# First attention of a three-layer block on one Trainium2 core: output products on two column halves, softmax weights normed by GpSimd before they are turned

## The chip, the cores and the metric

One core of one Trainium2 chip runs the whole program. The metric is the device time of one execution in microseconds (us), as the median of the runs. Engines are TensorE (PE in the profile, its weight loads PEld), VectorE (DVE), ScalarE (ACT), GpSimd (POOL) and SyncE (SP, which issues most transfers).

## The reference

256 tokens of width 1024, all in float32, pass through three layers. The change lies in the first one, an attention with 16 heads of 64 features and one shared key and value head (k and v of 64 features each, 256 keys):

```
q = rms_norm(proj_q per head);  k = rms_norm(proj_k);  v = proj_v
allowed = the 64 best keys by an indexer's score, in chunks not later than the query's
logits = (q . k) / 8 + rel_bias[t5_bucket(key - query)];  -1e30 where not allowed
p = softmax(logits);  out = p @ v;  h = h + out(256 x 1024) @ w_o
h = h + (relu(norm(h) @ w_up) ** 2) @ w_down
```

## The kernel before

**Blocks.** Tokens lie in two blocks of 128 rows. Queries of block 0 see only keys 0 to 127, those of block 1 all 256. So the softmax weights of one head are 128 x 384 numbers: 128 x 128 of block 0 and 128 x 256 of block 1, side by side in a buffer `P` (four heads deep), queries on the partitions.

**Per head.** TensorE makes the logits of two heads at a time (`logits_a`, L1079: row halves of 64 features, then a bf16 product that adds the mask). DVE adds the bias from `A["toep"]`, writes minus the logits to `P` and takes the row minimum in the same instruction (`min_a`, L2764). ACT takes the exponential in place, and its sum per row into `den` (L2037). TensorE turns three 128 x 128 blocks (L716, called from `turned`, L891) into a PSUM bank, 6 or 7 by turns. DVE copies them to `PT` (`turned`, L2720); ACT does so for heads 7, 10 and 13 (`act_turns`, L330). Then three products with the turned weights stationary and 64 value columns moving (L904 to L906) give the output with tokens on the partitions:

```
o0, o1 = psum[:, g % 2, at:at + 64], psum[:, g % 2, 256 + at:256 + at + 64]
nc.tensor.matmul(o0, pt[:, 0:128], vcol(0, h), start=True, stop=True)
nc.tensor.matmul(o1, pt[:, 128:256], vcol(0, h), start=True, stop=False)
ins = nc.tensor.matmul(o1, pt[:, 256:384], vcol(1, h), start=False, stop=True)
```

**Per group of four heads.** DVE takes the reciprocals of `den` and scales the group's output (`normed_out`, L2725). TensorE turns it (`out_turned`, L910), ACT makes the high half (`out_high`, L2017) and DVE the low half (`out_low`, L2734) of a two-part representation: each large product is made as three (high x high, high x low, low x high; L628 to L630). The product with w_o goes in four weight chunks wo0 to wo3; chunk j takes group j's output (`product`, L915).

**Order.** Every engine's program is written out by hand. TensorE's (`attention`, L888) takes logits two pairs ahead of the transposes, and spreads the first quarters of chunk wo0's product into the last heads. Engines meet by semaphores only; each engine runs its instructions in order.

**Weight chunks.** SP loads a chunk of 1 MB; its high half is made by ACT (L1769), or by GpSimd for the names in `pool_high` (wo1 and wo2 here), its low half by DVE (L2417) or GpSimd (L1726). GpSimd's program also scales the queries (`scale_queries`, L1690): the second half of them at the start of the attention. A chunk's buffer is loaded again once its low half is made.

**Other work around it.** TensorE makes a table `tab_c` (24 x 512) for a later layer at the start of the attention; ACT copies it out (L2060) and stores it, and issues, behind its last head (L2050, L1925), a 3 MB transfer that writes it shifted row by row to `skew_c` in HBM. The first MLP follows: its second kind of weights (`mlp0.d0`) is loaded once the low half of `mlp0.u0` is made.

**The dilated attention.** In the third layer's attention (L1419) the values are stationary, 64 columns to a head, two heads on the two column halves of the array, and the output has features on the partitions.

Of the kernel before, what the change touches and what calls it, by code (L numbers as in the profile page):

```python
# [23 lines left out]
P = 128  # L24
# [84 lines left out]
def program(nc, t):  # L109
# [8 lines left out]
    with ctx:  # L118
# [89 lines left out]
        for j in range(4):  # L208
            rows(f"wo{j}", kview(t["a_w_o"][0]), 2 * j, 2, D, lo="dve" if j == 3 else "pool")
# [120 lines left out]
        act_turns = {"A": (7, 10, 13), "B": (1, 7, 10, 13)}  # L330
# [76 lines left out]
        plan("a_exp_ready", [f"A.h{h}.exp" for h in range(16)])  # L407
        plan("b_row_max", [f"B.h{h}.max" for h in range(16)])
# [73 lines left out]
        def hidden_count(s, p, k):  # L482
# [9 lines left out]
             "score": area(8592, NB, SEQ), "P": area(9104, 4, 384), "PT": area(10640, 2, 384),  # L492
             "o": area(12304, 4, 512), "toep": area(14352, 16, SEQ)}
# [47 lines left out]
        hs, hd, hr = st[:, 8:40], st[:, 40:72], st[:, 72:104]  # L541
        mx, nmx, den, rden = st[:, 104:112], st[:, 112:120], st[:, 120:152], st[:, 152:184]
# [64 lines left out]
        def _(pe):  # L607
# [343 lines left out]

            logit_bank = (4, 5, 2, 3)
# [150 lines left out]
            def between_a(i, part):  # L1103
                if (i, part) == (1, 0):
                    query_transposes(1, (6, 7))
                if (i, part) == (2, 0):
                    wait_read("A.qT2")
                    wait_read("A.qT3")

            attention("A", logits_a, lambda s, h: A["kvw"][:, s, 64:128], "wo", between_a)  # L1110
# [522 lines left out]
        def _(pool):  # L1633
# [63 lines left out]

            for c in range(NC):
                if chunks[c]["name"] in ("wo0", "wo1"):
                    scale_queries(int(chunks[c]["name"][2]))  # L1700
                if chunks[c]["name"] == "dqb":
# [48 lines left out]
        def _(act):  # L1750
# [271 lines left out]
            def turned(L, h):  # L2022
                S = A if L == "A" else B
                act.wait_ge(*full[f"{L}.h{h}.T"])
                run(S["PT"][:, h % 2, :], psum[:, bank[f"{L}.h{h}.T"], 0:384], ACT.Copy, read[f"{L}.h{h}.T"])

            def heads(L, tag, between, behind=0):
                split_at = {"A": {6: 1, 10: 2}, "B": {5: 0, 8: 1, 11: 2}}[L]
                for h in range(16):
# [4 lines left out]
                    for blk, c0, w in ((0, 0, 128), (1, 128, 256)):  # L2034
                        at, c = (h // 4) * 8 + blk * 4 + h % 4, (h % 4) * 2 + blk
                        if L == "A":
                            run(A["P"][:, h % 4, c0:c0 + w], A["P"][:, h % 4, c0:c0 + w], ACT.Exp,  # L2037
                                done[f"A.h{h}.exp"] if blk else None, bias=mx[:, c:c + 1], scale=-1.0,
# [1198 lines left out]
```

## Time and profile before

| what | value |
|---|---|
| median of 3 runs | 1105.88 us (1105.83 to 1105.90) |
| the profiled execution's own time | 1105.73 us |
| its span | 1103.6 us |
| TensorE busy | 1090.9 us, 99% of the span |
| DVE, ACT, GpSimd busy | 757.8, 600.3, 149.6 us |
| granted TensorE clock over the span | 0.999 |
| first attention, from the first exponential to the third chunk of w_o | about 60 to 99 us |

The share of busy time is an average over the whole program. Matmuls are pipelined and their ends are modelled, so the way from one TensorE line to the next is read from starts; a product on f32 operands is recorded as two instructions.

### The profile page before, as it was taken

Reading aid. Unit: us, or ns where it says so; the run is one execution under the profiler, and the core shown is the slowest. Engines: PE = TensorE matmul, PEld = TensorE weight load, DVE = VectorE, ACT = ScalarE, POOL = GpSimd, SP = SyncE. Lnnn points to the kernel's source line nnn. Section 1 sums busy time; section 2 is a strip of 40 time slices with the busy share of each in tenths; the row PEclk is TensorE's granted clock in tenths of the full one; section 3 lists DMA queues with packets and bytes.
Section 4 is the critical chain, followed back from the end, with each engine's and each line's share of the span. In section 5 each row is a group of like instructions: output and inputs, shape, how many; then the busy total and the mean of one; then the engine's idle time right before and its main releaser. Section 6 shows DMA issues by size and latency. Waiting matters only on the chain.

```text
span 1103.6 us, 17798 instructions
## 1 busy us (share of the span) xinstructions
PE 1090.9 (99%) x6977; PEld 973.0 (88%) x6977; DVE 757.8 (69%) x1054; ACT 600.3 (54%) x788; POOL 149.6 (14%) x113
## 2 busy tenths in 40 slices
PE   8999999999999999999999999999999999999997
PEld 7868888888998888888889999898899989999997
DVE  6774665656668466656557878576587577988884
ACT  6574644444698464444455546555555357546454
POOL 4652000000377220000030000000000002000003
PEclk9999999999999999999999999999999999999999
DMA  9836565556433156565645654446653556545631
GB/s 303 289 117 123 188 223 191 191 190 233 138 106 129 33 161 217 187 195 189 200 154 191 191 158 144 131 153 231 201 166 121 168 214 229 200 176 196 226 136 39
DMA packets 138929, 194.00 MB, mean 176 GB/s; under 512 B 7163, under 2 KB 113112, under 8 KB 138860
## 3 DMA queue, kind: packets, MB, share of 16 engines
q1 hardware_dynamic: 129004, 184.02, 50.7%
q10 hardware_dynamic: 9248, 8.95, 3.2%
q8 instruction: 47, 0.77, 0.3%
q0 software_dynamic: 608, 0.08, 0.1%
q14 instruction: 22, 0.18, 0.0%
HBM read 191.90 MB, written 6.37 MB: 180 GB/s over the span
## 4 chain that ended last, share of the span: by engine, by line
PE 91%; ACT 4%; DVE 4%; issue 1%; DVEq 0%; ACTq 0%
PE psum L628 22%; PE psum L629 22%; PE psum L630 22%; PE psum L842 11%; PE psum L846 6%; ACT arena L1755 3%; PE psum L716 2%; PE psum L746 1%; PE psum L1392 1%; PE psum L1419 1%; DVE arena L2711 1%; DVE st L2710 1%; PE psum L1353 0%; PE psum L904 0%; PE psum L906 0%
## 5 line engine op out<-in xcount | busy, mean ns | idle before, releaser
L2417 DVE TENSOR_TENSOR wlo<-raw,whi 128x2048 fp32r<-128x2048 f32 (+1 forms) x134 | 302.4, 2264 | 134.8 <-ACT whi L1769 133.7
L1769 ACT ACTIVATE whi<-raw 128x2048 fp32r<-128x2048 f32 (+1 forms) x149 | 277.4, 1871 | 174.0 <-PE psum L630 126.3
L628 PE MATMUL psum<-xA,whi 128*128 128x256 f32 x840 | 239.2, 285 | 0.0
L630 PE MATMUL psum<-xA,wlo 128*128 128x256 f32 x840 | 237.6, 283 | 0.0
L629 PE MATMUL psum<-xA,whi 128*128 128x256 f32 x840 | 237.6, 283 | 0.0
L1726 POOL TENSOR_TENSOR wlo<-raw,whi 128x288 fp32r<-128x288 f32 (+3 forms) x43 | 81.8, 1930 | 746.5 <-ACT whi L1769 746.2
L628 PEld LDWEIGHTS psum<-xA,whi 128*128 128x128 f32 x840 | 160.3, 191 | 2.9 <-DVE wlo L2648 0.9
L629 PEld LDWEIGHTS psum<-xA,whi 128*128 128x128 f32 x840 | 160.4, 191 | 1.1
L630 PEld LDWEIGHTS psum<-xA,wlo 128*128 128x128 f32 x840 | 160.3, 191 | 0.1
L842 PE MATMUL psum<-xA,whi 128*128 128x512 f32 x512 | 122.5, 390 | 0.0
L628 PE MATMUL psum<-whi,xC 128*128 128x512 f32 (+1 forms) x296 | 114.5, 387 | 0.0
L629 PE MATMUL psum<-wlo,xC 128*128 128x512 f32 (+1 forms) x296 | 114.2, 386 | 0.0
L630 PE MATMUL psum<-whi,xC 128*128 128x512 f32 (+1 forms) x296 | 113.9, 385 | 0.0
L842 PEld LDWEIGHTS psum<-xA,whi 128*128 128x128 f32 x512 | 95.5, 188 | 20.7 <-DVE xA L2525 1.3
L628 PE MATMUL psum<-whi,xA 128*128 128x512 f32 (+1 forms) x256 | 99.9, 390 | 0.0
L630 PE MATMUL psum<-whi,xA 128*128 128x512 f32 (+1 forms) x256 | 98.3, 384 | 0.0
L629 PE MATMUL psum<-wlo,xA 128*128 128x512 f32 (+1 forms) x256 | 98.2, 384 | 0.0
L1890 ACT ACTIVATE arena<-psum 128x512 f32<-128x512 f32 x32 | 19.1, 597 | 96.1 <-PE psum L846 96.0
L846 PEld LDWEIGHTS psum<-xA,wlo 128*128 128x128 f32 x512 | 65.6, 191 | 2.5
L846 PE MATMUL psum<-xA,wlo 128*128 128x256 f32 x512 | 66.4, 283 | 0.0
L630 PEld LDWEIGHTS psum<-whi,xC 128*128 128x128 f32 x296 | 55.6, 188 | 10.8
L628 PEld LDWEIGHTS psum<-whi,xC 128*128 128x128 f32 x296 | 55.7, 188 | 9.8
(311 smaller groups left out, 1685.7 us busy)
## 6 DMA issues: line engine op xcount, KB each, us to landing
raw<-in_w_in SPq DMA_DIRECT2D x42, 1024.0 KB, 5.0
raw<-in_mlp_w_up SPq DMA_DIRECT2D x32, 1024.0 KB, 5.3
raw<-in_mlp_w_down SPq DMA_DIRECT2D x32, 1024.0 KB, 4.8
raw<-in_w_gate SPq DMA_DIRECT2D x11, 1024.0 KB, 5.2
raw<-in_w_up SPq DMA_DIRECT2D x11, 1024.0 KB, 6.4
down_raw<-in_w_down SPq DMA_DIRECT2D x6, 1024.0 KB, 8.1
arena<-in_w_down SPq DMA_DIRECT2D x5, 1024.0 KB, 8.3
raw<-in_b_w_o SPq DMA_DIRECT2D x4, 1024.0 KB, 5.0
```

The costliest lines, as they stand in the source:

```text
L628: nc.tensor.matmul(out, lh, rh, start=start, stop=False, skip_group_check=skip)
L629: nc.tensor.matmul(out, lh, rl, start=False, stop=False, skip_group_check=skip)
L630: return nc.tensor.matmul(out, ll, rh, start=False, stop=stop, skip_group_check=skip)
L716: ins = nc.tensor.transpose(out[0:m, n * P:n * P + P], src, ident[:, :])
L746: ins = nc.tensor.transpose(out[:, (2 * i + blk) * P:(2 * i + blk) * P + P], hres[:, blk, k * P:k * P + P], ident[:, :])
L842: nc.tensor.matmul(psum[:, 4 + 2 * j2 + nt, :], hi[:, k, nt * P:nt * P + P], xA[:, :, k, :], start=k == 0, stop=False)
L846: ins = nc.tensor.matmul(psum[:, 4 + 2 * j2 + nt, 0:SEQ], lo[:, k, nt * P:nt * P + P], xA[:, 0, k, :], start=False, stop=k == KT - 1)
L1726: ins = T(wlo[split_of[c]][:, at:at + step], raw_bufs[raw_of[c]][:, at:at + step], f(whi[split_of[c]][:, at:at + step]), ALU.subtract)
L1755: ins = nc.scalar.activation(out, in_, func, **kw)
L1769: nc.scalar.activation(whi[split_of[c]][:, 0:n], raw_bufs[raw_of[c]][:, 0:n], ACT.Copy).then_inc(hi_sem, 1)
L1890: nc.scalar.activation(half_buf[:, j2, :].rearrange("p (a b) -> p a b", b=SEQ), psum[:, 4 + 2 * j2:6 + 2 * j2, SEQ:512], ACT.Copy).then_in ...
L2417: V.tensor_tensor(wlo[split_of[c]][:, 0:n], raw_bufs[raw_of[c]][:, 0:n], f(whi[split_of[c]][:, 0:n]), ALU.subtract).then_inc(lo_sem["dve"], 1)
```

## The change

- The output products of the first attention keep the values stationary (128 x 64) and move the turned weights (256 columns of the first key block, 128 of the second). Even heads write partitions 0 to 63, odd heads 64 to 127. The output is feature-major at once, so its transposes and the scaled copy on DVE are gone.
- As tokens now lie along the columns, the weights are normed before they are turned: DVE takes the reciprocals of a pair (`weight_factor`), GpSimd scales `P` in place (`norm_weights`), two instructions a head. DVE does it all for heads 0 and 1.
- The turned weights of a pair are copied in one instruction of 128 x 768 from banks 6 and 7, by DVE, or by ACT for pairs 3, 5 and 7. `P` is six heads deep, `PT` four, the row minima eight.
- GpSimd splits wo1 in pieces between the pairs. It makes wo2's high half behind them; wo2's low half is DVE's.
- `tab_c` is copied by DVE instead of ACT. The transposes of the second half of the queries come ahead of head 0's. ACT's shifted store to `skew_c` stands behind its copy of pair 7.

The diff, cut to its core. First the chunk list, TensorE's program and GpSimd's:

```diff
-            rows(f"wo{j}", kview(t["a_w_o"][0]), 2 * j, 2, D, lo="dve" if j == 3 else "pool")
+            rows(f"wo{j}", kview(t["a_w_o"][0]), 2 * j, 2, D, lo="dve" if j >= 2 else "pool")
...
+        act_pairs = (3, 5, 7)
...
+            def attention_pairs(logits, value, tag, between):
+                def turned(h):
+                    if h % 2 == 0:
+                        open_bank(f"A.t{h // 2}", 7)
+                        pe.wait_ge(read_sem[6], uses[6])
+                    pe.wait_ge(*done[f"A.h{h}.nrm" if h > 1 else f"A.h{h}.first"])
+                    for n in range(3):
+                        ins = nc.tensor.transpose(psum[:, 6 + h % 2, n * P:n * P + P],
+                                                  A["P"][:, h % 6, n * P:n * P + P], ident[:, :])
+                    if h % 2:
+                        close_bank(ins, f"A.t{h // 2}")
...
+                def outputs(i):
+                    g, at, pair = i // 2, (i % 2) * 256, (2 * i, 2 * i + 1)
+                    if i % 2 == 0:
+                        open_bank(f"A.oT{g}", g % 2)
+                    wait_read(f"A.t{i}")
+                    for k, c0, w, p0 in ((0, 0, 256, 0), (1, 128, 128, 256)):
+                        for h in pair:
+                            r0 = (h % 2) * 64
+                            ins = nc.tensor.matmul(psum[r0:r0 + 64, g % 2, at + c0:at + c0 + w], value(k),
+                                                   A["PT"][:, h % 4, p0:p0 + w], start=k == 0, stop=k == 1,
+                                                   skip_group_check=True)
+                    if i % 2:
+                        close_bank(ins, f"A.oT{g}")
...
+                for i in range(7):
+                    between(i, 0)
+                    if i < 6:
+                        logits(i + 2)
+                    if i == 0:
+                        query_transposes(1, (0, 1))
+                    if i == 1:
+                        outputs(0)
+                    turned(2 * i)
+                    if i > 1:
+                        outputs(i - 1)
+                    turned(2 * i + 1)
+                    if i == 6:
+                        open_residual(tag, (0, 2))
+                        product(0, (0, 2))
+                turned(14)
+                outputs(6)
+                turned(15)
+                open_residual(tag, (1, 3))
+                product(0, (1, 3))
+                outputs(7)
+                product(1, (0, 1, 2, 3))
+                product(2, (0, 1, 2, 3))
+                last_residual_step(tag, "M0", xA, lambda j: read[f"A.oT{j}"])
...
+            def norm_weights(i):
+                pool.wait_ge(*done[f"A.rden{i}"])
+                for h in (2 * i, 2 * i + 1):
+                    for blk, c0, w in ((0, 0, 128), (1, 128, 256)):
+                        at = (h // 4) * 8 + blk * 4 + h % 4
+                        p = A["P"][:, h % 6, c0:c0 + w]
+                        ins = nc.gpsimd.tensor_scalar(p, p, rden[:, at:at + 1], None, ALU.mult)
+                        if blk:
+                            ins.then_inc(done[f"A.h{h}.nrm"][0], 1)
...
+            def weighted_heads():
+                c = split_started("wo1")
+                for i in range(1, 3):
+                    run(high_piece(c, 1024 * (i - 1), 1024))
+                    norm_weights(i)
+                for i in range(3, 7):
+                    ins = low_piece(c, 512 * (i - 3), 512)
+                    if i == 6:
+                        ins.then_inc(lo_sem["pool"], 1)
+                    norm_weights(i)
+                norm_weights(7)
+                c = split_started("wo2")
+                run(high_piece(c, 0, 1024))
+                run(high_piece(c, 1024, 1024), done["wo2.hi"])
...
```

ScalarE's program:

```diff
+            def turned_pair(i):
+                act.wait_ge(*full[f"A.t{i}"])
+                run(A["PT"][:, (2 * i) % 4:(2 * i) % 4 + 2, :], psum[:, 6:8, 0:384], ACT.Copy, read[f"A.t{i}"])
...
-                    if L == "A" and h - 2 in act_turns["A"]:
-                        turned("A", h - 2)
-                    if h - behind in (8, 12):
+                    if L == "A" and h % 2 and (h - 3) // 2 in act_pairs:
+                        turned_pair((h - 3) // 2)
+                    if L == "A" and h in (7, 11):
+                        out_high(L, (h - 7) // 4)
...
                 if L == "A":
+                    turned_pair(7)
                     act.wait_ge(s_tab, 32)
                     shift_rows(tab_c, skew_c, 24)
...
```

VectorE's program:

```diff
+            def turned_pair(i):
+                dve.wait_ge(*full[f"A.t{i}"])
+                if i not in act_pairs:
+                    run(V.tensor_copy(A["PT"][:, (2 * i) % 4:(2 * i) % 4 + 2, :], psum[:, 6:8, 0:384]), read[f"A.t{i}"])
...
+            def first_weights_normed(h):
+                dve.wait_ge(*done[f"A.h{h}.exp"])
+                run(V.reciprocal(rden[:, h:h + 5:4], den[:, h:h + 5:4]))
+                for blk, c0, w in ((0, 0, 128), (1, 128, 256)):
+                    p = A["P"][:, h, c0:c0 + w]
+                    run(V.tensor_scalar(p, p, rden[:, h + 4 * blk:h + 4 * blk + 1], None, ALU.mult),
+                        done[f"A.h{h}.first"] if blk else None)
+
+            def head_pairs(row_min, between):
+                for i in range(8):
+                    if i == 0:
+                        row_min(4)
+                        turned_pair(0)
+                        row_min(5)
+                    else:
+                        for h in (2 * i + 4, 2 * i + 5):
+                            if h < 16:
+                                row_min(h)
+                        turned_pair(i)
+                    if i < 7:
+                        weight_factor(i + 1)
+                    between(i)
+                    if i in (4, 6):
+                        out_low("A", (i - 4) // 2)
+                low_of("wo2")
+                out_low("A", 2)
+                low_of("wo3")
+                out_low("A", 3)
...
             min_a(2)
-            heads("A", min_a, between_a)
+            dve.wait_ge(*full["tab_c"])
+            run(V.tensor_copy(lrow_c, psum[0:24, bank["tab_c"], :]), read["tab_c"])
+            min_a(3)
+            first_weights_normed(0)
+            first_weights_normed(1)
+            head_pairs(min_a, between_a)
```

`weight_factor(i)` waits for the exponential of head 2i + 1 and takes the four reciprocals of pair i; `between` holds DVE's scaled copy of the fourth query tile at i = 0.

## Rows read from the trace of the kernel before

**Rows 1.** The page, chain that ended last: share of the span by engine.

```profile
PE 91%; ACT 4%; DVE 4%; issue 1%; DVEq 0%; ACTq 0%
```

**Rows 2.** Windows: us; busy us (instructions) of PE, PEld, DVE, ACT, POOL; clock, DMA, GB/s.

```profile
60.00:70.00 10.00, 8.76 (x71) 6.15 (x67) 6.98 (x27) 7.45 (x26) 9.65 (x7) 1.00 0.63 217
...
80.00:90.00 10.00, 10.00 (x78) 9.35 (x79) 6.50 (x20) 5.19 (x18) 0.00 (x0) 1.00 0.14 28
```

**Rows 3.** Timeline, transposes of heads 0 and 3: start us, us, engine, line, what.

```profile
61.35 0.55 PE L716 MATMUL psum<-ident,arena 128*128 128x128 f32 x3 [0.46 <-ACT arena L1755]
...
67.28 0.55 PE L716 MATMUL psum<-ident,arena 128*128 128x128 f32 x3
```

**Rows 4.** Timeline of one pair: logits, mask, transposes, DVE's copy, next transposes.

```profile
68.06 0.39 PE L906 MATMUL psum<-arena 128*128 128x64 f32 x2
...
68.37 0.93 PE L1087 MATMUL psum<-arena 64*128 64x128 f32 x8
...
69.23 0.50 PE L1091 MATMUL psum<-pick_mask,ident_bf 128*128 128x384 bf16 x2
...
69.57 0.49 PE L716 MATMUL psum<-ident,arena 128*128 128x128 f32 x3
...
70.16 0.56 DVE L2723 COPY arena<-psum 128x384 f32<-128x384 f32 x1 [0.64 <-PE psum L716]
...
70.61 0.55 PE L716 MATMUL psum<-ident,arena 128*128 128x128 f32 x3
```

**Rows 5.** Chain in order of time, the same transposes: end of chain step, us, line.

```profile
69.73 0.34 PE psum L716 x3
```

**Rows 6.** Timeline: transposes of heads 13 and 15, first wo2 product.

```profile
83.54 0.50 PE L716 MATMUL psum<-ident,arena 128*128 128x128 f32 x3
...
88.19 0.50 PE L716 MATMUL psum<-ident,arena 128*128 128x128 f32 x3
...
99.03 0.39 PE L628 MATMUL psum<-whi,xA 128*128 128x512 f32 x1
```

**Rows 7.** Timeline of the dilated attention: its output products on column halves.

```profile
802.70 2.17 PE L1419 MATMUL psum<-arena 128*64 128x256 f32 x24
804.71 0.61 PE L1425 MATMUL psum<-ident,st 128*64 128x128 f32 x8
```

**Rows 8.** Groups by form, whole program: count, busy us, mean ns, idle before.

```profile
L1721 POOL CAST whi<-landing 128x1024 fp32r<-128x1024 f32 x2 | 2.1, 1038 | 0.1
L1726 POOL TENSOR_TENSOR wlo<-raw,whi 128x512 fp32r<-128x512 f32 x16 | 19.9, 1276 | 24.1 <-ACT whi L1769 23.8
L2723 DVE COPY arena<-psum 128x384 f32<-128x384 f32 x25 | 13.9, 558 | 7.3 <-PE psum L716 6.7
L1755 ACT ACTIVATE arena<-psum 128x384 f32<-128x384 f32 x27 | 13.3, 491 | 16.2 <-PE psum L716 15.2 <-ACT arena L1755 0.5
L3027 DVE TENSOR_SCALAR arena<-arena,st 128x256 f32<-128x256 f32 x8 | 3.3, 413 | 0.3
L2769 DVE CUSTOM_DVE_ANT_0 arena<-psum,arena 128x256 f32<-128x256 f32 x16 | 6.8, 424 | 0.6
```

**Rows 9.** Timeline: skew_c transfer, load of mlp0.d0, its high half, its first product.

```profile
86.34 0.85 ACTq L1925 DMA_DIRECT2D skew_c<-tab_c  x1
...
105.94 0.37 SPq L1531 DMA_DIRECT2D raw<-in_mlp_w_down  x1
...
116.12 1.92 ACT L1769 ACTIVATE whi<-raw 128x2048 fp32r<-128x2048 f32 x1 [1.72 <-DMA raw<-in_mlp_w_down]
...
123.25 0.45 PE L628 MATMUL psum<-whi,xC 128*128 128x512 f32 x1
```

**Rows 10.** DMA queues (packets, MB, share) in 86.0:101.1, then 105.9:113.4; q10 is skew_c.

```profile
q10 hardware_dynamic: 1896, 1.94, 66.2%
...
q10 hardware_dynamic: 485, 0.49, 41.9%
q1 hardware_dynamic: 240, 0.81, 41.3%
```

More of the change, by code:

```diff
@@ L407, in program @@
         plan("a_exp_ready", [f"A.h{h}.exp" for h in range(16)])
+        plan("a_factor_ready", [f"A.rden{i}" for i in range(1, 8)])
+        plan("a_first_weights_normed", [f"A.h{h}.first" for h in range(2)])
+        plan("a_weights_normed", [f"A.h{h}.nrm" for h in range(2, 16)])
+        pool_high_ready = plan("pool_high_ready", ["wo2.hi"])
         plan("b_row_max", [f"B.h{h}.max" for h in range(16)])
@@ L1700, in _ @@
                     scale_queries(int(chunks[c]["name"][2]))
+                if chunks[c]["name"] == "wo1":
+                    weighted_heads()
+                    continue
                 if chunks[c]["name"] == "dqb":
@@ L2022, in turned @@
             def turned(L, h):
[L2023 removed]
                 act.wait_ge(*full[f"{L}.h{h}.T"])
[L2025 removed]
+                run(B["PT"][:, h % 2, :], psum[:, bank[f"{L}.h{h}.T"], 0:384], ACT.Copy, read[f"{L}.h{h}.T"])
+            def turned_pair(i):
+                act.wait_ge(*full[f"A.t{i}"])
+                run(A["PT"][:, (2 * i) % 4:(2 * i) % 4 + 2, :], psum[:, 6:8, 0:384], ACT.Copy, read[f"A.t{i}"])
             def heads(L, tag, between, behind=0):
[L2028 removed]
+                split_at = {"A": {}, "B": {5: 0, 8: 1, 11: 2}}[L]
                 for h in range(16):
@@ L2036, in heads @@
                         if L == "A":
-                            run(A["P"][:, h % 4, c0:c0 + w], A["P"][:, h % 4, c0:c0 + w], ACT.Exp,
-                                done[f"A.h{h}.exp"] if blk else None, bias=mx[:, c:c + 1], scale=-1.0,
+                            c = (h % 8) * 2 + blk
+                            run(A["P"][:, h % 6, c0:c0 + w], A["P"][:, h % 6, c0:c0 + w], ACT.Exp,
+                                done[f"A.h{h}.exp"] if blk else None, bias=row_mins[:, c:c + 1], scale=-1.0,
                                 accum_out=den[:, at:at + 1])
@@ L2055, in between_a @@
             def between_a(h):
-                if h == 2:
+                if h == 3:
                     query_turned(2)
                 if h == 4:
-                    act.wait_ge(*full["tab_c"])
-                    run(lrow_c, psum[0:24, bank["tab_c"], :], ACT.Copy, read["tab_c"])
+                    act.wait_ge(*read["tab_c"])
                     act.dma_start(tab_c.ap(), lrow_c).then_inc(s_tab, 16)
@@ L2414, in low_part @@
             def low_part(c, hi_value=None):
-                dve.wait_ge(hi_sem, high[c] if hi_value is None else hi_value)
+                if c == index["wo2"]:
+                    dve.wait_ge(*done["wo2.hi"])
+                else:
+                    dve.wait_ge(hi_sem, high[c] if hi_value is None else hi_value)
                 n = chunks[c]["n"]
```

57 lines of the change are left out of this document (34 added, 23 removed).

## The prediction

> **What bounds the kernel now.** I read the page first: TensorE carries 91% of the chain that ended last, and the profiled execution spans 1103.6 us [rows 1]. It took 1105.73 us by its own time, so 2.1 us lie around the span, and it stands 0.15 us under the median of the runs shown. The sum below is made against 1105.73. A measurement of this kernel can tell about 0.2% (2.2 us) from no change.
>
> Then the windows of the first attention, which runs from about 60 to 99 us. The reader is to see two things [rows 2]: TensorE has gaps in the first ten microseconds (8.76 busy of 10) and none between 80 and 90, and its granted clock is 1.00 (2.4 GHz) in both. So in its steady part the attention is bound by TensorE's own instruction stream, and what is taken from that stream is worth its time, as long as nothing else comes to stand in front of it.
>
> Then the timeline of one pair of heads [rows 4]. Logits and mask take from 68.37 to 69.57 (1.20 us; 1.29 with the 0.09 that lie before them, the last of two output records having started at about 68.17 and each taking 0.11). From 69.57 to 70.61 come three transposes, 0.34 on the chain [rows 5], and a head's three output products: 0.70. Products of 64 columns at 0.23 us each pay for loading 128x128 transposed weights, not for columns. A pair costs 1.29 + 0.67 + 1.37 (six products) = 3.3 us, and the stream from the transposes of head 3 (67.28, [rows 3]) to those of head 13 (83.54, [rows 6]) takes 16.26 us for five pairs.
>
> **The change, part by part.**
>
> Outputs on column halves. The products at 802.70 in the dilated attention have the new form: 12 of them, two heads on two column halves, 6 of 256 and 6 of 128 columns, in 2.01 us to the next line at 804.71 [rows 7]. That is 2304 columns at 0.87 ns. A pair of the first attention has 2 x 256 + 2 x 128 = 768 columns: 0.67 us. I add 0.09 on either side for the change of tile form, since the logits, which also change it, start 0.09 us after the last output product: 0.86 us for a pair against 1.37. Eight pairs give 8 x 0.51 = 4.1 us less on TensorE. The Trainium skill (TensorEngine Tiling (Array Packing), Key Properties) says that a change of the tiling mode drains the engine. The logits' own exit costs 0.22 us (0.64 by 768 columns, against 0.86 until the mask at 69.23); at 0.22 on either side the term would be 2.1 us less. I keep 0.09, the one gap that stands between two tile forms without a mask behind it, and leave the 2.1 to the range.
>
> The outputs come out feature-major, so the four blocks of output transposes go, 0.45 us each (four transposes at 0.11 [rows 5]), 1.8 us. The output norm on DVE (four reciprocals and four 128x512 products) goes too; it was never on TensorE's path, so nothing.
>
> In all TensorE would issue 5.9 us less. This is what would come if nothing were late.
>
> The start. DVE now copies the table rows (about 0.7), takes the row minimum of head 3 (0.8; the 256-column part is 0.42, [rows 8]), and norms heads 0 and 1 itself: a reciprocal (some 0.2) and two scalings, 0.41 and about 0.29 [rows 8], 1.0 us a head with gaps. Queued from 60.4, that puts the first transposes at 62.9 instead of 61.35 and head 1's at 63.9. Behind them stand a pair copy, a row minimum, the factor and the GpSimd norm of heads 2 and 3: head 3's transposes come to 68.2, against 67.28 [rows 3]. Loss 0.9 us.
>
> The new wait. In DVE's program the factor of pair i+1 stands behind the copy of pair i, and the copy behind the last transposes of pair i. GpSimd norms only after the factor, and the transposes of pair i+1 wait for GpSimd. So a loop goes round once a pair. From the start of a pair's last transposes: 0.59 us until the copy starts (69.57 to 70.16, [rows 4]); the copy of 768 columns 0.96 (0.56 for 384, at 1.04 ns a column more, [rows 8]); factor 0.25 (an estimate: a few columns, and the way between two engines); 0.08 to GpSimd; GpSimd's first head G; 0.05; then transposes 0.34 and outputs 0.86 on TensorE before the next last transposes. TensorE can put only the logits (1.29) under the middle of it. G has no row. Bounds: a cast has 1.04 us for 1024 columns, a two-input operation 1.28 for 512 [rows 8]. By the cast (one input, as here) with 0.18 fixed, 128 and 256 columns are 0.29 + 0.40 = 0.7; by the two-input line 0.45 + 0.72 = 1.2; 0.5 if two instructions overlap. I take 0.7, since the new operation reads one tensor. The loop is then 0.59 + 1.0 + 0.25 + 0.08 + 0.7 + 0.05 + 0.34 + 0.86 = 3.87 us where DVE copies (pairs 0, 1, 2, 4, 6). Where ACT copies (3, 5, 7) DVE only waits for the transposes, the 1.0 falls out and the ACT copy (about 0.85, from 0.49 for 384 columns, [rows 8]) lies beside the norm: TensorE's own stream binds, 2.87 us. From head 3 to head 13: 4.1 + 3.87 + 2.87 + 3.87 + 2.87 = 17.6 us (the first has 0.25 more, DVE being behind with the fourth query tile). Before: 16.3. So head 13's transposes start at 85.8 instead of 83.54: 2.2 us late, where TensorE's stream alone would have been early.
>
> The end of the attention. From head 13's transposes to the third weight product (wo2) the stream before took 99.03 - 83.54 = 15.5 us [rows 6]. In the new one there is no wait left, since the first half product (2.7 us) lies over the last norm: 0.34 + 2.73 + 0.34 + 0.86 + 0.34 + 2.73 + 0.86 + 5.46 = 13.7. Gain 1.8 us.
>
> GpSimd's and DVE's other work. The split of wo1 is spread between the norms: 1.1 to 1.3 us a piece, against 1.5 to 2.5 us in which GpSimd waits each turn; nothing. It is whole before the second product. The low part of wo2 moves to DVE, 2.3 us behind GpSimd's 2.1 us of high part: ready about 5 us after head 15's transposes, needed 9.4 after; nothing. ACT's split of wo3 keeps its place.
>
> So wo2's product starts 0.4 us later than before (2.2 - 1.8).
>
> The skewed bias rows. ACT issues the 3 MB transfer of skew_c at 86.34, 12.7 us ahead of wo2's product [rows 6, 9]. In the new program it stands behind the copy of pair 7, 1.5 us after head 15's transposes instead of 1.85 before them (88.19), and the stream from there is shorter: 8 us ahead. It moves 4.7 us closer to the first down weights of the MLP, whose load is issued at 105.94 behind a release that keeps its distance to wo's products. That load takes 10.2 us now because the tail of skew_c is still moving: 0.49 MB of it beside 0.81 MB of weights from 105.9 on [rows 10]. With 4.7 us less of a start, 1.2 MB are left instead. And there is no slack: the weights land at 116.12, and ACT's half, DVE's half, the square and its low part follow on, and TensorE takes them up at 123.25 without a gap [rows 9]. In the shared stretch the weights move at about 0.16 MB/us, which brings the megabyte through in 8 to 11 us. I take 1.0 us of delay; the bounds are nothing, and 4.7 if the load had to wait out the whole shift.
>
> Sum: 0.9 + 1.3 - 1.8 + 1.0 = 1.4 us; 1105.73 + 1.4 = 1107.1, beside the median about 1107.2. I give **1107.1**, 0.1% more: no change that can be told.
>
> **Rivals.**
>
> B, TensorE's saving comes whole. If the loop were shorter than I read it (the copy starting earlier, G at 0.5), TensorE's 5.9 us less would stand against 0.9 at the start and 1.0 of the transfer: 1101.7. For it: the last windows show TensorE bound [rows 2]. Against it: 0.59 and the copy's slope are read directly, and G at 0.5 alone gives 1.0 of the loop back (1106.1). Chance 0.15.
>
> C, GpSimd becomes the bound, on the other side. The place is the norm of the first head of a pair; it decides from G = 0.9 on. At the two-input price of 1.2 each loop, ACT's too, grows by 0.5, and so does the start: 6 x 0.5 = 3.0 us, 1110.1. For it: all GpSimd arithmetic in this trace but the casts goes at that price. Against it: the casts, with one input, take half. The Trainium skill (GPSIMD Engine Reference, When to use GPSIMD) calls GpSimd the wrong place for elementwise work, about twice VectorE's time for two inputs and near line rate for one; DVE's 0.41 for 256 columns beside the cast's slope agrees with the second half, and the first half is this rival. Chance 0.22.
>
> D, the bias rows collide with the down weights for most of the shift: 3 to 4.7 us of delay instead of 1.0, 1109 to 1110.8. For it: 10.2 us now against no slack at 123.25. Against: in the shared stretch the weights moved faster than the bias rows. Chance 0.12.
>
> E, the column halves don't run beside each other after transposes of the whole array: 1.4 us a pair, 1110.5. The rows at 802.70 speak against it. Chance 0.03. A fall of the granted clock in the new gaps is in none of them: at 8.76 of 10 it stayed at 1.00 [rows 2].
>
> **How the numbers follow.** Forecast 0.48, B 0.15, C 0.22, D 0.12, E 0.03. Its own range is 1105.2 to 1108.2. B gives most of faster (0.17 with a little of the forecast's edge), C, D and E nearly all of slower (0.35), the rest is the same, 0.48. The range leaves out B's end and the worst of C with D together: 1103.4 to 1110.5.
>
> **What would show it.** Outputs: a pair of heads near 0.86 us between transposes; more than 1.2 is E. The loop: TensorE idle about 1.0 us ahead of the first transposes of pairs 2, 3 and 5 (behind a GpSimd instruction), and none to speak of ahead of 4 and 6; if none anywhere, it is B. G: GpSimd's 256-column norm near 0.4; near 0.7 is C. Head 13's transposes near 85.8, wo2's product near 99.4. The transfer: the down weights land 11 us after issue and TensorE waits about 1 us before the first down product. The prediction is wrong if head 13's transposes start before 84.

## The result, and the profile after

The changed kernel takes 1118.39 us (median of 4 runs, 1117.59 to 1118.63) against 1105.89 us: ratio 1.0109, 95% interval 1.0096 to 1.0122. It is slower by 12.5 us, outside the range. The profiled execution took 1118.37 us and spans 1116.6 us.

The page, chain by engine, answers to [rows 1]. GpSimd and the DMA are new on it:

```profile
PE 87%; DVE 4%; ACT 4%; POOL 2%; issue 1%; DMA 1%; DVEq 0%; ACTq 0%; POOLq 0%
```

The timeline of TensorE, transposes of heads 0, 1, 3, 13 and 15, the wo2 product and the first down product, answers to [rows 3, 6, 9]. The first number is the start in us:

```profile
63.99 0.52 PE L966 MATMUL psum<-ident,arena 128*128 128x128 f32 x3 [0.57 <-DVE arena L2852]
...
64.81 0.55 PE L966 MATMUL psum<-ident,arena 128*128 128x128 f32 x3 [0.30 <-DVE arena L2852]
...
70.80 0.44 PE L966 MATMUL psum<-ident,arena 128*128 128x128 f32 x2 [0.87 <-POOL arena L1765]
...
95.40 0.90 PE L966 MATMUL psum<-ident,arena 128*128 128x128 f32 x3
...
101.24 0.55 PE L966 MATMUL psum<-ident,arena 128*128 128x128 f32 x3
...
110.88 0.39 PE L634 MATMUL psum<-whi,xA 128*128 128x512 f32 x1
...
136.57 0.47 PE L634 MATMUL psum<-whi,xC 128*128 128x512 f32 x1 [1.31 <-DVE xC L2721]
```

That splits the loss (starts after minus starts before, each stretch less the one ahead of it):

| stretch | before | after | change | forecast |
|---|---|---|---|---|
| to head 3's transposes | 67.28 | 70.80 | +3.5 | +0.9 |
| head 3 to head 13 | 16.26 | 24.60 | +8.3 | +1.3 |
| head 13 to the wo2 product | 15.49 | 15.48 | 0.0 | -1.8 |
| wo2 to the first down product | 24.22 | 25.69 | +1.5 | +1.0 |

The sum is 13.3; the spans differ by 13.0. Half a microsecond of the first row is there before the changed part begins (the logits of head 1 start at 56.92 instead of 56.42). Behind the first down product nothing is lost.

One turn of the loop where DVE copies, pairs 4 and 5 (heads 8 to 11), in the timeline of the four engines (to be held beside [rows 4]):

```profile
86.24 0.55 PE L966 MATMUL psum<-ident,arena 128*128 128x128 f32 x3
...
89.81 0.52 PE L966 MATMUL psum<-ident,arena 128*128 128x128 f32 x3 [1.74 <-POOL arena L1765]
90.26 0.87 PE L980 MATMUL psum<-arena 128*64 128x256 f32 x8
91.20 0.55 PE L966 MATMUL psum<-ident,arena 128*128 128x128 f32 x3
...
94.01 0.52 PE L966 MATMUL psum<-ident,arena 128*128 128x128 f32 x3 [2.25 <-POOL arena L1765]
...
86.90 0.96 DVE L2839 COPY arena<-psum 128x768 f32<-128x768 f32 x1 [1.47 <-PE psum L966]
87.89 0.18 DVE L2845 RECIPROCAL st<-st 128x4 f32<-128x4 f32 x1
...
91.84 0.18 DVE L2845 RECIPROCAL st<-st 128x4 f32<-128x4 f32 x1 [1.45 <-issue]
...
88.17 2.98 POOL L1765 TENSOR_SCALAR arena<-arena,st 128x128 f32<-128x128 f32 x4 [0.74 <-DVE st L2845]
91.11 1.27 POOL L1773 TENSOR_TENSOR wlo<-landing,whi 128x512 fp32r<-128x512 f32 x1
92.36 2.99 POOL L1765 TENSOR_SCALAR arena<-arena,st 128x128 f32<-128x128 f32 x4
```

From 86.24 to 91.20 the reader can add: 0.66 to the copy, 0.99 for it, 0.28 for the factor and the way to GpSimd, 1.49 for head 10's scaling (half of 2.98), 0.15 to the transposes, 0.45 for them, 0.94 for the outputs: 4.96 us where 3.87 stood. The odd head's scaling ends almost on the same path: GpSimd is done with head 11 at 88.17 + 2.98 = 91.15, 0.05 ahead of its transposes. From 91.20 to 95.40, where ACT copies, it is 4.20 where 2.87 stood: there the copy falls out (4.96 - 0.99 = 3.97), and GpSimd's piece of wo1, running until 92.38, holds the scaling up by another 0.2. The outputs are busy for 0.87, about the 0.86 forecast; they are not at fault.

The windows of after show a second loss, which [rows 2] don't have (columns as there; the last three are granted clock, DMA share and GB/s):

```profile
68.00:70.00 2.00, 0.52 (x3) 0.31 (x3) 1.81 (x9) 1.38 (x6) 2.00 (x4) 1.00 0.00 0
70.00:72.00 2.00, 1.20 (x9) 1.03 (x11) 0.54 (x1) 1.47 (x6) 1.73 (x2) 0.82 0.00 0
72.00:74.00 2.00, 1.69 (x8) 0.35 (x4) 1.03 (x5) 0.00 (x0) 1.20 (x2) 0.50 0.02 4
...
76.00:78.00 2.00, 2.00 (x13) 1.18 (x11) 0.26 (x1) 1.06 (x3) 1.01 (x1) 0.50 0.00 0
...
88.00:90.00 2.00, 0.26 (x3) 0.22 (x3) 1.83 (x9) 1.13 (x5) 1.83 (x3) 1.00 0.00 0
...
92.00:94.00 2.00, 0.00 (x0) 0.02 (x1) 0.02 (x1) 1.90 (x6) 2.00 (x4) 1.00 0.00 0
94.00:96.00 2.00, 1.96 (x15) 1.38 (x15) 0.00 (x0) 0.94 (x4) 1.34 (x2) 0.79 0.00 0
96.00:98.00 2.00, 2.00 (x7) 1.61 (x6) 1.53 (x3) 0.00 (x0) 0.33 (x1) 0.50 0.00 0
```

Twice, behind a gap (0.52 busy of 2 us, then 0.00 of 2), the granted clock falls to 0.50, the lower of its two levels (1.2 GHz). The Trainium skill (TensorE: Matmul & The Clock Gate, Part 1) says that an engine left idle is taken down to that level; these rows agree on the level. They don't show that every such gap is followed by a fall: from 88 to 90 us the engine was busy for 0.26 us, and the clock stayed at 1.00 up to 94.

### The profile page after: what moved, and what is told of

Read it like the earlier page. It is cut to its first block, busy times and chain, and to the rows that moved or that the text cites. A ratio compares the mean times of both kernels' runs of the same rounds, so it can differ in the third digit from the quotient of the medians.

```text
span 1116.6 us, 17718 instructions
## 1 busy us (share of the span) xinstructions
PE 1092.1 (98%) x6929; PEld 967.1 (87%) x6929; DVE 757.7 (68%) x1053; ACT 600.5 (54%) x787; POOL 166.4 (15%) x143
## 4 chain that ended last, share of the span: by engine, by line
PE 87%; DVE 4%; ACT 4%; POOL 2%; issue 1%; DMA 1%; DVEq 0%; ACTq 0%; POOLq 0%
PE psum L634 21%; PE psum L635 21%; PE psum L636 21%; PE psum L848 10%; PE psum L852 5%; ACT arena L1858 3%; PE psum L722 1%; POOL arena L1765 1%; DMA raw<-in_mlp_w_down 1%; PE psum L1452 1%; PE psum L1479 1%; ACT whi L1872 1%; PE psum L752 1%; DVE arena L2823 1%; DVE st L2822 1%
## 5 line engine op out<-in xcount | busy, mean ns | idle before, releaser
L634 PEld LDWEIGHTS psum<-whi,xC 128*128 128x128 f32 x296 | 55.7, 188 | 11.3 <-issue 1.5
```

The lines of the kernel that those rows point to most:

```text
L634: nc.tensor.matmul(out, lh, rh, start=start, stop=False, skip_group_check=skip)
```

## The experiments

Theory 1 was that GpSimd's scaling stands in a ring through each pair at twice the price taken. The rivals were a late factor, the copy, the clock and the bias rows. The runs are called m1 and e1 to e12, the changed kernel's profile is called after. A ring is a chain of waits that comes back to its start once a pair.

**GpSimd's price by itself (m1)**, in the kernel before, at 77 to 90 us, where GpSimd is idle.

```diff
+for n in (128, 256, 384, 512, 1024): tensor_scalar(to[:, 0:n], from[:, 0:n], column, mult)
+for n in (128, 256): tensor_scalar(... 0.5 ...), tensor_tensor of 2 x n with a repeated factor, tensor_copy, tensor_tensor
```

> The kernel before, with single GpSimd instructions on scratch columns added in GpSimd's idle time behind the splits of wo2 (75 to 100 us): a scaling by a column of scalars at 128, 256, 384, 512 and 1024 columns, by a constant at 128 and 256, a product of two tensors with one broadcast along the columns at 2x128 and 2x256, a copy at 128 and 256, a product of two whole tensors at 128 and 256. It measures the disputed price by itself. Theory 1 (the scaling by a column is dear in itself): 0.60 and 0.92 us at 128 and 256 columns here too, with nothing else going on, and the slope of a two-input operation or worse. Rival (it is dear in the changed kernel only because VectorE and GpSimd share a way into SBUF): 0.3 and 0.4 us here, near the copy. The broadcast product should take about 0.6 and 1.04 us. The time of the kernel stays at 1105.9.

Measured, groups by form (mean ns of one is the number behind the bar's second comma):

```profile
L1705 POOL TENSOR_SCALAR arena<-arena,st 128x256 f32<-128x256 f32 x1 | 0.9, 930 | 0.1
...
L1705 POOL TENSOR_SCALAR arena<-arena,st 128x128 f32<-128x128 f32 x1 | 0.6, 606 | 0.0
L1707 POOL TENSOR_SCALAR arena<-arena 128x128 f32<-128x128 f32 x1 | 0.5, 530 | 0.1
...
L1712 POOL COPY arena<-arena 128x256 f32<-128x256 f32 x1 | 0.4, 402 | 0.1
L1712 POOL COPY arena<-arena 128x128 f32<-128x128 f32 x1 | 0.3, 292 | 0.1
```

A copy costs 0.29 + 0.40 = 0.7 us, the figure taken from the cast. Scaling by a column costs 0.61 + 0.93 = 1.54 us, more than a product of two tensors (0.45 + 0.73); with a constant for the column 0.53 + 0.86. So reading one tensor is not what makes the cast cheap. The Trainium skill (GPSIMD Engine Reference, When to use GPSIMD) calls work with one input on GpSimd roughly line-rate. Here that holds for the copy alone: 256 columns in 0.40 us, where DVE's scaling took 0.41 [rows 8] and GpSimd's takes 0.93.

**The scaling left out (e1), and cut to one column (e2).** The first leaves out the scaling of heads 2 to 15, the second all but the first column of each block.

```diff
-pe.wait_ge(*done[f"A.h{h}.nrm" if h > 1 else f"A.h{h}.first"])
+pe.wait_ge(*done[f"A.h{h}.exp" if h > 1 else f"A.h{h}.first"])
...
 def norm_weights(i):
+    return
```

```diff
-p = A["P"][:, h % 6, c0:c0 + w]
+p = A["P"][:, h % 6, c0:c0 + 1]
```

> The changed kernel without GpSimd's norm of heads 2 to 15: the softmax weights of these heads stay unnormed, and TensorE's transposes wait for the exponential instead. Theory 1 (the norm is what was lost): TensorE's stream binds, about 2.9 us a pair; head 13's transposes start near 80 us of the span instead of 95.4, and the time is about 1102 to 1103 us, with the load of the first down weights still 1 to 2 us late. Rival (the clock, or the pair copies and the order of VectorE's queue, hold TensorE back without any norm): 1108 us or more.

> The changed kernel with every wait and every GpSimd instruction of the norm, but each scales one column instead of 128 or 256; the other weights stay unnormed. Theory 1 (the loop is as predicted and only GpSimd's duration was mis-sized): with about 0.3 us an instruction a head costs 0.6, the loop is near the predicted 3.9 and 2.9 us, and the time is the predicted one, 1106 to 1108 us. Rival (the order of the queues is what costs, whatever the norm takes): above 1112 us. Second rival (gaps of 1 us a pair already halve the clock): above 1110 us, with the granted clock under 1.0 in the stretch from 70 to 100 us.

Measured 1108.77 us (ratio 1.0024, 1.0015 to 1.0034) and 1109.23 us (1.0028, 1.0018 to 1.0038). Between 9 and 10 us go, so the scaling is the main cause. In the second a head's scaling takes 0.52 us (1.04 for four instructions), and TensorE still waits 4.8 us in all for GpSimd ahead of its transposes. From head 3 (about 68.7) to head 13 (86.46) it is 17.8 us. The forecast's 17.6, worked out again with 0.52 for 0.7 in its three turns with a copy by DVE, would be 17.1: at such a price the ring is within 0.7 us of the one foretold. The clock stays at 1.00 from 60 to 112 us, so gaps of 0.8 to 1.3 us did not lower it. Its time still lies 1.2 us above the 1106 to 1108 expected, and the first missed its 1102 to 1103 us by 6. The timeline of DVE and GpSimd in the first says why:

```profile
64.15 2.05 DVE L2845 TENSOR_SCALAR arena<-arena,st 128x128 f32<-128x128 f32 x2
66.23 0.17 DVE L2842 RECIPROCAL st<-st 128x2 f32<-128x2 f32 x1
66.44 2.34 DVE L2845 TENSOR_SCALAR arena<-arena,st 128x128 f32<-128x128 f32 x2
...
63.91 2.14 POOL L1763 CAST whi<-landing 128x1024 fp32r<-128x1024 f32 x2
66.14 4.99 POOL L1766 TENSOR_TENSOR wlo<-landing,whi 128x512 fp32r<-128x512 f32 x4
```

DVE's scaling of heads 0 and 1 takes 2.05 and 2.34 us while GpSimd runs (the first ends at 66.20, the casts at 66.05); alone it took 0.68. GpSimd, freed of the weights, had moved its splits beside DVE. Head 3's transposes then start near 73.4. From there to head 13's it is 15.0 us.

**No scaling at all (e5)**: also DVE's of heads 0 and 1 left out.

```diff
 def first_weights_normed(h):
     run(V.reciprocal(...))
+    return
     for blk, c0, w in ((0, 0, 128), (1, 128, 256)):
```

> The changed kernel with no scaling of the weights at all, neither GpSimd's nor DVE's of the first two heads (the outputs are left unnormed); the factors of pairs 1 to 7 are still formed. In the run with only GpSimd's scaling left out, DVE's two scalings of the first heads took 2.05 and 2.34 us instead of 0.68 us beside GpSimd's splits of the next weights, TensorE waited 1.35 and 1.97 us for them and its clock was 0.50 of full in 70 to 72 us. Theory (that stretch is why the run missed its 1102 to 1103 us): without them the third head's transposes start before 69 us, no clock below 1.00 from 60 to 100 us, and 1102 to 1104.5 us. Rival (the pair loop is no shorter than the loop before even without a scaling, because of DVE's copies or the bank pair): 1106 us or more, with waits for DVE copies ahead of outputs in each pair.

Measured 1104.39 us, ratio 0.9982 (0.9972 to 0.9991), at the edge of the 1102 to 1104.5 expected. This bounds the idea: with a scaling that costs nothing the new shape gives 1.7 us, and 1.28 us of wait for the down weights stand against it. In steady pairs TensorE takes 2.9 us (odd heads' transposes at 72.19, 75.13 and 78.02), as forecast (2.87), but the stretch from head 3 (67.8) to head 13 (84.22) still takes 16.4 us: TensorE has new waits for the pair copies. In the program one pair of PSUM banks carries all transposes, and one copy frees both, which is likely why; no run changed that. The timeline of TensorE:

```profile
70.91 0.55 PE L966 MATMUL psum<-ident,arena 128*128 128x128 f32 x3 [1.19 <-DVE arena L2832]
...
82.94 0.55 PE L966 MATMUL psum<-ident,arena 128*128 128x128 f32 x3 [0.96 <-ACT arena L1851]
```

**The factors first (e3).** DVE forms the factors of pair i+1 ahead of the copy of pair i.

```diff
-                        turned_pair(i)
-                    if i < 7:
-                        weight_factor(i + 1)
+                        if i < 7:
+                            weight_factor(i + 1)
+                        turned_pair(i)
```

> The changed kernel with VectorE's reciprocals of pair i+1 ahead of its copy of pair i, so that GpSimd's norm of the next pair runs under the transposes and the copy of this one. Nothing is left out. Theory 1: GpSimd itself binds now, 2.98 us of norm and 1.27 of split a pair, 4.3 us against 4.9 on average before; the time falls by about 3 us, to 1115. Rival (the order of VectorE's queue was the cause): the loop opens and the time falls below 1109.

Measured 1113.26 us, ratio 1.0061 (1.0044 to 1.0078). The copy leaves the ring and 5 us go, 2 more than expected. What is left is GpSimd itself, busy without a pause, in these windows of it (GpSimd is the fifth busy time):

```profile
80.00:82.00 2.00, 1.16 (x10) 0.44 (x8) 0.75 (x5) 1.90 (x6) 2.00 (x4) 1.00 0.00 0
82.00:84.00 2.00, 1.79 (x14) 1.10 (x14) 0.89 (x5) 1.50 (x5) 2.00 (x3) 1.00 0.00 0
```

2.98 us of scaling and a 1.27 us piece of wo1 make a turn of 4.2 us (transposes of heads 6, 8 and 10 at 77.94, 82.14 and 86.34). Now GpSimd is the bound, without any ring.

**A cheaper scaling (e4).** A pair in two products of two tensors, the factors repeated.

```diff
-for h in (2 * i, 2 * i + 1): for blk ...: tensor_scalar(P[:, h % 6, c0:c0 + w], rden[:, at:at + 1])
+for blk ...: tensor_tensor(P[:, h % 6:h % 6 + 2, c0:c0 + w], up2(rden[:, at:at + 2], w))
```

> The changed kernel with the GpSimd scaling of a pair written as two multiplies of two tensors, one for each query block of both heads, the factors repeated along the columns, instead of four multiplies by a column. The same is computed. In the run of the kernel before with added GpSimd instructions these forms took 0.62 and 1.04 us against 0.61 and 0.93 us twice each, so 1.7 instead of 3.0 us a pair. Theory 1 (the scaling's own duration stands on the path of each pair): 7 x 1.3 us go, and the two stretches at half clock (4 to 5 us) shrink or go with the gaps: 1106 to 1110 us, transposes of head 15 at 91 to 94 us instead of 101.2. Rival (the wait is for the factor, which DVE gives late behind a pair copy, and the duration only fills a part of it): the gaps stay, above 1114 us.

Measured 1116.69 us, ratio 1.0093 (1.0069 to 1.0117). A pair costs 1.61 us instead of 2.98, and next to nothing comes of it: 1106 to 1110 was wrong. The turns at full clock, from even head to even head, say why:

```profile
80.88 0.52 PE L966 MATMUL psum<-ident,arena 128*128 128x128 f32 x3 [1.55 <-POOL arena L1765]
...
84.79 0.52 PE L966 MATMUL psum<-ident,arena 128*128 128x128 f32 x3 [0.82 <-POOL arena L1765]
...
89.70 0.52 PE L966 MATMUL psum<-ident,arena 128*128 128x128 f32 x3 [1.82 <-POOL arena L1765]
```

They take 3.91 and 4.91 us, where 4.20 and 4.96 stood. Only the first head's 1.49 us were in the ring; the second head's lay beside transposes and outputs (1.39 us), and now both must end before the first transposes, 1.61. The 7 x 1.3 us expected had counted hidden time. Since both heads are ready at once, the next transposes come 1.25 us later (82.13, forecast 0.34 + 0.86 = 1.20) and not 1.39, which gives back the 0.12 that 1.61 costs over 1.49.

**The bias rows earlier (e6).** ScalarE issues skew_c ahead of head 12's exponential.

```diff
+                if h == 12:
+                    act.wait_ge(s_tab, 32); shift_rows(tab_c, skew_c, 24)
...
                     turned_pair(7)
-                    act.wait_ge(s_tab, 32)
-                    shift_rows(tab_c, skew_c, 24)
```

> The changed kernel with ScalarE issuing the second table's shifted transfer ahead of the exponentials of head 12 instead of behind the last pair copy (some 10 us earlier, to an idle time of the DMA engines). Theory (the transfer runs beside the load of the first down weights, which then comes 1 to 1.5 us late and leaves a wait of 1.3 us ahead of the first down product): the wait goes, -1.0 to -1.5 us. Rival (the load is late from its own start and the product's wait comes from DVE's low part): the wait stays, within 0.4 us of the changed kernel.

Measured 1117.28 us, ratio 1.0091 (1.0075 to 1.0108) against 1.0109. In after, the timeline shows the transfer's issue, the load's, and its landing, where ACT waits for it:

```profile
102.72 0.85 ACTq L2028 DMA_DIRECT2D skew_c<-tab_c  x1
...
117.86 0.37 SPq L1591 DMA_DIRECT2D raw<-in_mlp_w_down  x1
...
129.47 1.92 ACT L1872 ACTIVATE whi<-raw 128x2048 fp32r<-128x2048 f32 x1 [3.21 <-DMA raw<-in_mlp_w_down]
```

and with the transfer issued earlier:

```profile
87.46 0.85 ACTq L2028 DMA_DIRECT2D skew_c<-tab_c  x1
...
118.34 0.37 SPq L1591 DMA_DIRECT2D raw<-in_mlp_w_down  x1
...
126.63 1.90 ACT L1872 ACTIVATE whi<-raw 128x2048 fp32r<-128x2048 f32 x1
```

The weights are split 8.3 us after issue instead of 11.6, and the wait of 1.31 us is gone. The trace shows that; the two times alone don't, as their intervals overlap.

**The gaps filled (e7).** Eight transposes of the identity into unused columns ahead of each even head's wait.

```diff
+if h > 1 and h % 2 == 0:
+    for _ in range(8): nc.tensor.transpose(psum[:, 6, 384:512], ident[:, :], ident[:, :])
 pe.wait_ge(*done[f"A.h{h}.nrm" ...])
```

> The changed kernel with eight transposes of the identity into unused columns of the pair's first bank, ahead of the wait for each even head's scaled weights (heads 2 to 14). They take about 0.8 us of TensorE's time in gaps of 1 to 2 us. Theory (the clock fell to half after the gaps at 68 to 70 and 92 to 94 us, in stretches of 3 to 6 us): the granted clock stays 1.00 from 60 to 105 us, and the time falls by 2 to 4.5 us to 1114 to 1116.5 us. Rival (the clock falls for another reason, or such transposes don't count): the clock's rows stay as they are, and the time is the same or up to 5 us more where the transposes don't fit in the gaps.

Measured 1115.95 us, ratio 1.0086 (1.0069 to 1.0103). Its windows:

```profile
72.00:78.00 6.00, 5.07 (x41) 3.38 (x40) 3.46 (x15) 2.35 (x8) 4.75 (x6) 1.00 0.01 3
...
90.00:96.00 6.00, 4.80 (x32) 3.50 (x31) 1.61 (x4) 3.00 (x9) 4.03 (x6) 1.00 0.00 0
```

The clock stays at 1.00 (2.4 GHz), and 2.4 us go although the kernel issues 56 transposes more. From head 3 (70.51) to head 13 (93.85) it is 23.3 us instead of 24.6. That is what the ring gives at full clock by the turns above: 3 x 4.96 + 2 x 4.20 = 23.3.

**Two edits (e8), then four (e9) together**, and the first heads' scaling as products of two tensors alone (e10).

```diff
 e8:  pair scaling + factors first
 e9:  e8 + skew_c ahead of head 12 + the line below
 e10: the changed kernel + the line below
-run(V.tensor_scalar(p, p, rden[:, h + 4 * blk:h + 4 * blk + 1], None, ALU.mult), ...)
+run(V.tensor_tensor(p, p, rden[:, h + 4 * blk:h + 4 * blk + 1].to_broadcast([P, w]), ALU.mult), ...)
```

> The two edits together that each moved the time little: the scaling of a pair in two multiplies of two tensors (1.61 us a pair), and DVE forming the next pair's factors ahead of the copy of the present pair. The same is computed. Theory 1 (a ring ran through each pair: copy of the pair 1.0, factors 0.2, scaling, transposes with outputs between 1.8; in the run with the short scaling alone it stood at 3.9 and 4.9 us a pair, and in the run with the factors first GpSimd was busy 2.00 of every 2 us): either edit leaves the other's bound, and both together leave TensorE's own work of 2.9 us a pair: head 15's transposes at 89 to 91 us, no stretch below full clock, 1105 to 1107 us. Rival (a third thing bounds the pair, DVE's minima and copies or the six weight buffers): 3.5 us a pair or more, above 1109 us.

> As the run before, and two more edits: DVE scales the first two heads by a multiply of two tensors in place of a multiply by a column, and ScalarE issues the second table's shifted transfer ahead of head 12. The same is computed. Theory: 0.6 us less at the start, since such a multiply is not held by GpSimd's cast beside it, and 1.1 to 1.3 us less ahead of the first down product: 1103 to 1105.5 us, so 0 to 3 us less than the kernel before. Rival (with the pair loop at TensorE's own work the start is set by the exponentials, and the loads come late anyway): no less than the run before, and no less than the kernel before.

> The changed kernel with DVE's scaling of the first two heads as multiplies of two tensors with a repeated factor. Theory (the multiply by a column from and to SBUF waits for GpSimd's running instruction: 1.26 us beside the cast instead of 0.68): each head's scaling takes 0.7 to 0.8 us whether GpSimd runs or not, head 0's transposes come 0.4 to 0.5 us earlier, and the time falls by no more than that, as head 2's transposes wait for GpSimd. Rival (any instruction of DVE on SBUF is held): 1.2 us again for the one beside the cast.

Measured: e8 1111.39 us, ratio 1.0040 (1.0028 to 1.0052); e9 1110.14 us, 1.0029 (1.0020 to 1.0038); e10 1119.04 us, 1.0102 (1.0086 to 1.0117). Both edits of the ring together do what neither did, but not as much as the 1105 to 1107 us expected of e8 and the 1103 to 1105.5 of e9: from head 3 to head 13 e8 takes 20.2 us (with the clock at 0.50 in 76 to 78), e9 19.2 at full clock. The longest waits left in e9 stand ahead of heads 4 and 12:

```profile
72.56 0.52 PE L966 MATMUL psum<-ident,arena 128*128 128x128 f32 x3 [2.19 <-POOL arena L1765]
...
86.59 0.52 PE L966 MATMUL psum<-ident,arena 128*128 128x128 f32 x3 [2.15 <-POOL arena L1765]
```

In e10 the product of two tensors beside the cast takes 1.39 us for head 0 and 0.75 for head 1; it is held as the scaling by a column was (1.26 in after), so its theory falls:

```profile
63.90 1.39 DVE L2852 TENSOR_TENSOR arena<-arena,st 128x128 f32<-128x128 f32 x2
...
63.65 1.04 POOL L1770 CAST whi<-landing 128x1024 fp32r<-128x1024 f32 x1
```

**Orders changed, without (e11) and with filled gaps (e12).** Both have e4's scaling. The factors stand ahead of the next minima, head 5's minimum ahead of the first copy, skew_c behind head 15's exponential; then transposes ahead of heads 4 and 12.

```diff
+                        if 1 < i < 7:
+                            weight_factor(i + 1)
                         for h in (2 * i + 4, 2 * i + 5): row_min(h)
                         turned_pair(i)
...
+if h in (4, 12):
+    for _ in range(8): nc.tensor.transpose(psum[:, 6, 384:512], ident[:, :], ident[:, :])
```

> The changed kernel with the scaling of a pair in two multiplies of two tensors, and three orders changed: DVE forms the factors of the next pair ahead of the next minima (and the sixth head's minimum ahead of the first pair copy), and ScalarE issues the second table's shifted transfer behind head 15's exponential, ahead of the last pair copy. The same is computed. Theory (in the run of four edits the factors of pair 2 came 1.3 us after their exponential since two minima stood ahead, and the transfer's issue of 0.85 us stood ahead of heads 12 and 13): the waits ahead of heads 4 and 12 go from 2.2 us to about 1 us, and the time is 1105 to 1108 us, 1.5 to 3 us below the run of four edits. Rival (ScalarE's exponentials and copies, 2.9 us a pair on the mean, set the pairs, whatever DVE's order): within 1 us of the run of four edits, 1108 to 1111 us.

> The same, with eight transposes of the identity into unused columns ahead of the waits of heads 4 and 12 (0.8 us in gaps of 1 to 2 us). Theory (those gaps are what loses the clock in a part of the runs): the spread of the runs narrows to 3 us, the median falls by 0.5 to 1.5 us against the run before, granted clock 0.997 or more in the runs. Rival (the spread comes from elsewhere, the stretch at 10 to 20 us of the start among them): the same median and spread as the run before, or up to 0.8 us more.

Measured 1110.19 us (1107.85 to 1113.42), ratio 1.0036 (1.0022 to 1.0050), and 1110.55 us (1108.69 to 1110.88), 1.0034 (1.0021 to 1.0047). The order is worth nothing that can be told: e11 is where e9 was, not at the 1105 to 1108 us expected, and the waits have other releasers (1.91 us now for DVE's copy ahead of head 10). A pair now asks ScalarE for 2.3 us of exponentials and 0.6 of copies and high parts on the mean, GpSimd for 1.61 + 1.27, and TensorE for 2.9. Three engines equally full would mean that any wait is lost; this is argued from the sums, no run isolates it. With the filling the runs spread over 2.2 us (5 runs) instead of 5.6 (9 runs), and the median stayed. Windows of the two kernels, without and with it:

```profile
84.00:88.00 4.00, 2.86 (x14) 1.73 (x14) 1.79 (x10) 1.30 (x4) 1.61 (x2) 0.52 0.00 0
```

```profile
84.00:88.00 4.00, 2.86 (x26) 2.01 (x24) 1.89 (x10) 2.27 (x8) 1.61 (x2) 1.00 0.02 4
```

No version with the whole computation beat the kernel before.

## Why the prediction was wrong

**The outputs: right.** 0.86 us a pair forecast, 0.87 busy; by starts, which don't depend on modelled ends, e4 gives 1.25 - 0.34 = 0.91. With 0.22 on either side they would have taken 1.1.

**The end of the attention: right in shape.** 13.7 us were forecast from head 13 to the wo2 product. After took 15.48; but from head 13 to 15 after took 5.84 us, and e9, at full clock there, 4.36. Less that 1.5 it is 14.0.

**The bias rows: right.** The transfer stands 8.2 us ahead of wo2's product (8 forecast), the weights landed 11.6 us after issue (11), and TensorE waited 1.31 us (1.0). The earlier issue took the wait away.

**The start: mis-sized.** Heads 0 and 1 came at 63.99 and 64.81 for 62.9 and 63.9: 0.5 was there before, and 0.6 is DVE's scaling held beside the cast, which the text did not price. Head 3 at 70.80 for 68.2 is the next point.

**The failed step is G.** "By the cast (one input, as here)" gave 0.7, bounds 0.5 to 1.2. It is 1.49, above both. In a turn with DVE's copy that is 0.8 of the 1.1 us too much; the rest is spread over the other terms, none off by more than 0.11. Where ACT copies the step "the 1.0 falls out ... TensorE's own stream binds, 2.87 us" fails with it: with 1.49 the ring is 3.9 to 4.0 without the copy, and GpSimd's piece adds the rest. The term "GpSimd's and DVE's other work ... nothing" fails there too: with 2.98 us of scaling and a piece of 1.27 GpSimd has no time left in a turn of 4.20. At full clock the loop is 23.3 instead of 17.6: 5.7 us. At the start, heads 2 and 3 both are scaled in 3.0 us before head 3's transposes, some 1.6 us more than by G = 0.7. Rival C had the mechanism and its place, but its price of 1.2 came from splits, and its 3.0 us were about a quarter of the 11.3 us by which the time missed the forecast.

**"A fall of the granted clock in the new gaps is in none of them": wrong.** [rows 2] showed 1.2 us of gaps in ten; the new ones are up to 2 us in two. It cost 1.3 us of the loop and 1.5 at the end, and filling the gaps gave 2.4 back.

Together: 2.6 (start) + 5.7 + 1.3 (loop) + 1.8 (end) + 0.5 (down weights) = 11.9 over the forecast's 1.4, where the spans say 11.6.

**Rival B had no ground.** With no scaling at all 16.4 us stand between heads 3 and 13 against 16.26 before. The text took from its loop that TensorE's stream binds as soon as the copy is out; the waits for the pair copies (1.19 and 0.96 us in e5) were not in it.

What stays open: why scaling by a column costs GpSimd more than a product, and whether a scaling on another engine would do, or GpSimd without its pieces of wo1 between the pairs. Neither was tried.

## What to carry to other kernels

Price an operation by a row of the same operation; one of the same number of inputs is no stand-in. Where the price is bounded by rows of other operations, let the range reach beyond both. Before moving work to an idle engine, write down the ring of waits that it closes, term by term, and then ask again for each turn which term binds; a cheaper instruction gains only what lies in the ring. A gap of 2 us on TensorE can cost more than its length: two of those in after were followed by a lower clock, the one at 88 to 90 us was not.

## What was not expected of the hardware

- GpSimd: 128 and 256 columns f32 in 0.29 and 0.40 us as a copy, 0.45 and 0.73 as a product of two tensors, 0.61 and 0.93 as a scaling by a column.
- DVE's work from and to SBUF is held while GpSimd runs: 0.68 us became 1.26, 2.05 and 2.34, and the product of two tensors 1.39 for 0.75. The minima, which read PSUM and SBUF, kept 0.29 and 0.42 us beside GpSimd. The Trainium skill (SBUF — State Buffer, Who interferes with whom) has one port pair of the two, held for a whole instruction, and counts both forms, the scaling in a two-port mode and two inputs in SBUF, among those that take it; these rows agree.
- The times of the kernel before fell in two groups in the later comparisons: 1105.4 to 1106.4 us at a mean clock of 0.999, and 1107.0 to 1108.1 at 0.997. The one profile of the upper kind that has this kernel's program up to 77 us is m1's (1107.54 us, 0.997): the clock is 0.66 in its 10 to 12 us and 0.50 in 12 to 14. The profile of the kernel before has 1.00 there. Changed kernels show both (0.83 over 10 to 20 us in e8, 1.00 in e9), so starts of different profiles can be held against each other only less this step: head 0's transposes start at 63.22 us in m1 against 61.35 before, and at 65.27 in e8 against 63.58 in e11.
